# Layer 1's last k-tile and three of layer 0's four k-tiles of the experts' down product in three passes

## The reference

```python
h2 = modulate(rmsnorm(x, norm2_g[l]), sh2, sc2)        # layer 0: context rows too
eidx, w = route(h2, router_w, router_b)
out[tokens of e] += w * ((silu(xblk @ w1[e]) * (xblk @ w3[e])) @ w2[e])

def route(h, router_w, router_b):
    s = sigmoid(h @ router_w)                          # (tokens, 16 experts)
    sb = s + router_b
    gscore = top_k(sb.reshape(n, 4, 4), 2)[0].sum(-1)  # the two best of each group of 4
    # the best group; of its experts the two best, weighted by s
```

## Time and profile before

| | us |
|---|---|
| median of 3 runs (lowest to highest) | 3127.07 (3122.99 to 3132.42) |
| the profiled execution | 3131.46 |
| its span, first to last instruction | 3129.7 |
| mean granted TensorE clock | 0.982 |
| PE busy in the span | 3004.1 (96%) |
| DVE busy | 1785.8 (57%) |
| POOL, ACT busy | 946.6, 929.6 |

### The profile page before, as it was taken

One profiled execution on the slowest core, in us unless ns is written; L12 is line 12 of the kernel. 1 busy time (PEld: TensorE's weight loads), 2 busy tenths in 40 slices (PEclk: granted clock), 3 DMA queues, 4 the chain that ended last, 5 costly groups with the idle time before them and its releaser, 6 DMA issues. The chain is left out here.

```text
span 3129.7 us, 47079 instructions
## 1 busy us (share of the span) xinstructions
PE 3004.1 (96%) x16162; PEld 2410.8 (77%) x16163; DVE 1785.8 (57%) x2568; ACT 929.6 (30%) x1766; POOL 946.6 (30%) x559
## 2 busy tenths in 40 slices
PE   7999899999999989999998999899999998899998
PEld 4887788888888777777776888788888877666665
DVE  5473377858863677535574666365233247899540
ACT  4321265111212342222222422255222134222222
POOL 0050000002222236656574023000012213578664
PEclk9999999999999989999999999999999998999999
DMA  6122342434434448767786512242111144989653
GB/s 274 58 88 78 97 132 88 150 101 148 140 98 184 147 162 275 228 195 238 242 309 224 196 73 91 68 147 76 42 51 51 61 168 165 352 326 375 232 181 81
DMA packets 163516, 499.86 MB, mean 160 GB/s; under 512 B 30634, under 2 KB 83082, under 8 KB 139020
## 3 DMA queue, kind: packets, MB, share of 16 engines
q1 hardware_dynamic: 117288, 393.08, 34.0%
q0 software_dynamic: 17568, 59.82, 8.3%
q10 hardware_dynamic: 28516, 45.03, 4.5%
HBM read 421.76 MB, written 76.44 MB: 159 GB/s over the span
## 5 line engine op out<-in xcount | busy, mean ns | idle before, releaser
L225 PE MATMUL wide<-part,part 128*128 128x512 f32 (+2 forms) x2480 | 972.6, 392 | 18.1 <-DVEq L2552 5.6
L227 PE MATMUL wide<-part,part 128*128 128x512 f32 (+2 forms) x2480 | 950.8, 383 | 0.0
L226 PE MATMUL wide<-part,part 128*128 128x512 f32 (+2 forms) x2480 | 950.6, 383 | 0.0
L225 PEld LDWEIGHTS wide<-part,part 128*128 128x128 f32 x2480 | 469.1, 189 | 116.6 <-issue 22.0
L227 PEld LDWEIGHTS wide<-part,part 128*128 128x128 f32 x2480 | 468.6, 189 | 92.4
L226 PEld LDWEIGHTS wide<-part,part 128*128 128x128 f32 x2480 | 469.3, 189 | 90.5 <-issue 4.8
L1992 POOL TENSOR_TENSOR place<-place,place 128x512 f32 (+3 forms) x80 | 123.1, 1539 | 1019.7 <-DVE place L1939 1019.7
L3060 DVE TENSOR_TENSOR part<-place,part 128x2048 fp32r<-128x2048 f32 x118 | 331.7, 2811 | 4.0
L225 PE MATMUL bank<-part,part 128*128 128x512 f32 (+1 forms) x884 | 327.4, 370 | 3.3 <-DVE part L3080 3.3
L227 PE MATMUL bank<-part,part 128*128 128x512 f32 (+1 forms) x884 | 315.8, 357 | 0.0
L226 PE MATMUL bank<-part,part 128*128 128x512 f32 (+1 forms) x884 | 315.5, 357 | 0.0
(11 more groups left out here) (319 smaller groups left out, 3988.5 us busy)
## 6 DMA issues: line engine op xcount, KB each, us to landing
place<-in_w SPq DMA_DIRECT2D x148, 1024.0 KB, 5.1
place<-in_w SPq DMA_DIRECT2D x22, 2048.0 KB, 10.1
place<-in_ada_w ACTq DMA_DIRECT2D x72, 512.0 KB, 3.8
place<-in_w_gates SPq DMA_DIRECT2D x32, 640.0 KB, 5.0
place<-in_bias SPq DMA_DIRECT2D x96, 192.0 KB
place<-in_ada_w SPq DMA_DIRECT2D x6, 2048.0 KB, 17.4
place<-in_w_rows SPq DMA_DIRECT2D x6, 2048.0 KB, 9.8
place<-in_w_gates SPq DMA_DIRECT2D x16, 768.0 KB
```

The lines of the kernel that those rows point to most:

```text
L225: pe.matmul(out, left[0], right[0], start=first, stop=False)
L226: pe.matmul(out, left[0], right[1], start=False, stop=False)
L227: return pe.matmul(out, left[1], right[0], start=False, stop=last)
```

## The change

- Down products: layer 0 has one plain k-tile and three split ones (before two and two), layer 1 three plain and one split (before four plain). `plain_tiles` and `down_parts` give the numbers and the places.
- With it layer 1 gets layer 0's machinery: `load_second` on SP, `split_second` on DVE (once behind `leave_second`, then behind each expert's four pieces), the second copy on ACT, `leave_gated` on POOL, and its order on PE (gated transposes ahead of the slots').
- In layer 0 `load_second` and `split_second` handle 3 tiles (1.5 MB, 128x3072), in layer 1 one tile (0.5 MB, 128x1024).
- End of layer 0: `scale1` is made ahead of the last two of three pieces of next-layer weights, which now both wait for PE's last down product.
- The load of the second block's token list moves from SP to the head of ACT's queue.
- `keep_turning` ahead of layer 1's `turn(0)`: 10 instead of 40.
- Router: the two best of a group are found with fewer chained DVE operations; `rank` issues its product with the counts of earlier tiles ahead of the wait for the present ones; the first block's rows lose the raw copy.

```diff
-                keep_turning(s, pe, banks[4], 40)
+                keep_turning(s, pe, banks[4], 10)
...
-                do(dve.tensor_tensor(hi, g[:, :, 0:2], g[:, :, 2:4], ALU.max))
-                do(dve.tensor_tensor(both, g[:, :, 0:2], g[:, :, 2:4], ALU.add))
-                do(dve.tensor_tensor(top, hi[:, :, 0], hi[:, :, 1], ALU.add))
-                do(dve.tensor_tensor(mark, both[:, :, 0], both[:, :, 1], ALU.max))
-                do(dve.tensor_tensor(top, top, mark, ALU.max))
...
+                dve.tensor_tensor(sums[:, :, 4:6], twice[:, :, 0:2], twice[:, :, 2:4], ALU.add)
+                do(dve.tensor_tensor(sums[:, :, 0:4], twice[:, :, 0:4], twice[:, :, 1:5], ALU.add))
+                do(dve.tensor_reduce(top, sums, AX.X, ALU.max))
...
+def plain_tiles(last):
+    return 3 if last else 1
+def down_parts(s, last):
+    n = DE // P - plain_tiles(last)
+    at = A_W13 + 32768 + 2 * plain_tiles(last) * D
+    return s["place"](at, n, D), s["part"](at, n, D), s["part"](at + n * D, n, D)
...
             def load_second(e, before):
                 sp.wait_ge(s_y, before * 2 + 2)
                 apart(sp, s_sp)
-                sp.dma_start(down_raw, s["a"]["w2"][layer, e][:, 2:4]).then_inc(s_down, 16)
+                sp.dma_start(down_raw, s["a"]["w2"][layer, e][:, PLAIN:]).then_inc(s_down, 16)
...
-                if e >= 2 and not last:
+                if e >= 2:
                     load_second(e - 1, before)
...
             leave_second()
+            if last:
+                dve.wait_ge(s["first_w2"], 32)
+                split_second(1)
...
-                    if not last:
-                        dve.wait_ge(s_down, (e - 1) * 16 + 16 * n)
-                        split_second(e + n)
+                    dve.wait_ge(s_down, (e - 1) * 16 + 16 * n)
+                    split_second(e + n)
...
-                    if i:
-                        dve.wait_ge((s_room, s_ended)[i - 1], 1)
-                    if i == 2:
+                    if i == 1:
                         scale_next()
+                        dve.wait_ge(s_room, 1)
+                        dve.wait_ge(s_ended, 1)
```

More of the change, by code:

```diff
@@ L2082, in mix_and_route @@
     w13 = place(A_W13, 2, 2 * KD, DE)
-    w2 = place(A_W13 + 32768, 2, DE // P, D)[:, 0] if last else place(A_W13 + 32768, 2, 2, D)[:, 0]
-    w2_second = place(A_W13 + 36864, 2, D)
+    w2, w2_second = place(A_W13 + 32768, 2, plain_tiles(last), D)[:, 0], down_parts(s, last)[0]
     s_w0 = sem("w13_loaded")
@@ L2175, in _ @@
                 sp.wait_ge(s_xb[0], 16)
-            sp.dma_start(w2, s["a"]["w2"][layer, 0][:, 0:4 if last else 2]).then_inc(s["first_w2"], 16)
-            if not last:
-                sp.dma_start(w2_second, s["a"]["w2"][layer, 0][:, 2:4]).then_inc(s["first_w2"], 16)
+            sp.dma_start(w2, s["a"]["w2"][layer, 0][:, 0:plain_tiles(last)]).then_inc(s["first_w2"], 16)
+            sp.dma_start(w2_second, s["a"]["w2"][layer, 0][:, plain_tiles(last):]).then_inc(s["first_w2"], 16)
             if last:
@@ L2414, in _ @@
             act.wait_ge(s_fhi, 4)
[L2415 removed]
+            act.wait_ge(s_fx, 2)
         @block.vector
@@ L2685, in experts @@
     g2 = [place(at + 2 * DE, DE), place(A_W13 + 40960, DE)]
[L2686 to L2689, removed]
+    PLAIN = plain_tiles(last)
+    gtlo, gthi = part(at + 3 * DE, 4, P), part(A_W13 + 41472 if last else at + 2 * DE, DE // P - PLAIN, P)
+    down_a = place(A_W13 + 32768, 2, PLAIN, D)
+    down_raw, down_lo, down_hi = down_parts(s, last)
     plan = s["plan"]
@@ L2696, in experts @@
     s_whi, s_split = sem("w13_hi"), sem("w13_split")
[L2697 to L2700, removed]
+    s_down, s_dhi, s_dsplit, s_glo = sem("w2_second_loaded"), sem("w2_second_hi"), sem("w2_second_split"), \
+        sem("gated_lo")
+    s_ended = sem("products_passed")
     s_xb = s["slots_loaded"]
@@ L2757, in load_w2 @@
             def load_w2(e):
[L2758 to L2761, removed]
+                sp.dma_start(down_a[:, e % 2], s["a"]["w2"][layer, e][:, 0:PLAIN]).then_inc(s_w2[e % 2], 16)
             def load_second(e, before):
@@ L2797, in _ @@
                 if e == 1:
-                    sp.wait_ge(s["first_w2"], 16 if last else 32)
+                    sp.wait_ge(s["first_w2"], 32)
                     sp.sem_inc(s_w2[0], 16)
@@ L2808, in _ @@
             follow_w2(EXP - 1, older)
-            if not last:
-                done = sp.value_load(plan[0:1, PLAN_BEFORE + EXP:PLAN_BEFORE + EXP + 1], min_val=0, max_val=MAXB + 2)
-            if not last:
+            done = sp.value_load(plan[0:1, PLAN_BEFORE + EXP:PLAN_BEFORE + EXP + 1], min_val=0, max_val=MAXB + 2)
+            if last:
+                load_second(EXP - 1, done)
+            else:
                 for s_product in (s_h1, s_h3):
@@ new lines, in down @@
+                split = pe.snap(e + 1)
+                pe.wait_ge(s_dsplit, split)
+                pe.wait_ge(s_glo, r * 2 + (b + 1))
+                for h in range(2):
+                    cols = slice(h * 512, (h + 1) * 512)
+                    for k in range(PLAIN, DE // P):
+                        mm = split_product(pe, banks[6 + h][:], (gthi[:, k - PLAIN, :], gtlo[:, k, :]),
+                                           (down_hi[:, k - PLAIN, cols], down_lo[:, k - PLAIN, cols]), False,
+                                           k == DE // P - 1)
@@ L3009, in copy_gated @@
                 act.activation(gt.rearrange("p a b -> p (a b)"), banks[4][:], ACT.Copy).then_inc(s_gc, 1)
-                if not last:
-                    act.activation(gthi.rearrange("p a b -> p (a b)"), banks[4][:, 256:512], ACT.Copy).then_inc(s_gc, 1)
+                act.activation(gthi.rearrange("p a b -> p (a b)"), banks[4][:, PLAIN * P:512], ACT.Copy).then_inc(s_gc, 1)
             def copy_y(r, b):
@@ L3026, in body @@
                     silu(r * 2 + (b + 1))
[L3027 to L3028 removed]
                     copy_gated(r, b)
[L3030 to L3031 removed]
+                    copy_turned(0, b, r * 2 + (b + 2))
                     copy_h3(r * 2 + (b + 1))
@@ L3204, in body @@
                 for b in range(2):
-                    if not last:
-                        leave_gated(r, b)
+                    leave_gated(r, b)
                     leave_turned(0, b, r * 2 + (b + 2))
@@ L3216, in _ @@
             R = pool.snap(used // 2)
-            if not last:
-                leave_gated(R, 0)
+            leave_gated(R, 0)
             add_block(R, 0)
```

91 lines of the change are left out of this document (35 added, 56 removed).

## The result

| | before | changed |
|---|---|---|
| median | 3128.74 us (4 runs) | 3169.49 us (4 runs, 3167.79 to 3177.46) |
| ratio, 95% interval | | 1.0138 (1.0124 to 1.0153) |
| profiled execution's span | 3129.7 | 3167.8 |
| PE busy | 3004.1 | 2999.4 |
| DVE busy | 1785.8 | 1868.9 |

The medians lie 41 us apart, the profiled spans 38; the ratio, of the means, stands for 43. The direction was right, the size wrong by 30 us; 3169 lies outside the range of 3121 to 3152. In the span PE is busy 5 us less and idle 43 us more, and part of its busy time runs slower.

The account below looks back on a forecast made before the run. PE bound the kernel, with DVE full where layer 1's single-block experts follow each other. -10.0 + 15.0 + 1.9 - 8.2 + 14.0 - 1.6 = + 11.1 us took the median from 3127.07 to 3138, range 3121 to 3152.

Parts of the forecast that it names:

- What PE saves: Down products: 0.36 us saved per block, -10.0 us over layer 0's 28 blocks and -8.2 over layer 1's 23.
- behind an expert of two or three blocks nothing is lost, 10 of 15 times: Layer 0: split parts ready 12.1 us after their tiles' issue (T), PE wanting them at 13.7, so no wait.
- - 3.5 us, three such places: Layer 0, behind single-block experts 3, 7 and 11: PE waits 3.5 us each for the split parts.
- + 4.5 more: Layer 0, parts of expert 13, second single in a row: PE waits 5.4 us, 4.5 more than before.
- The clock: PE at half clock after long waits: three could cost 1.5 us each, counted only in the upper bound.
- high end: Upper bound, sum + 22 us: slower half MB, longer tile split and subtraction (+ 5 and + 3), and the clock.
- waits 14: Layer 1: PE waits near 14 us for DVE's pieces, at experts 3 to 6 and 10, 11; sum + 14.0.
- They still come ahead of DVE: Layer 1: SP's pieces, issued up to 13 us later, still land before DVE reaches them, at T + 6 earliest.
- Rival 3: Layer 1: transfers become the bound, nine singles losing 1 to 2 us more each, 3151 us; chance 0.15 with the clock.
- Rival 1: DVE's disturbance by POOL shrinks as PE slows, half of 29 us of waits goes, 3124 us; chance 0.25.
- Router and idle products: Router and start: -0.8 us per layer, -1.6; fewer idle products at layer 0's end give 1 within + 1.9.
- rival 2: DVE hides everything, only PE's work counts: -18.2 - 1.6 - 3 (idle products), 3104 us; chance 0.08.

Follow-up runs that it names:

- e6: Changed kernel, POOL's low-part subtraction cut to 8 of each tile's 128 columns in both layers: layer 0's stage 495.3 us against the changed kernel's 507.7.
- e4: Changed kernel, DVE making parts of only two of layer 0's three split tiles from the second expert on: layer 0's stage 487.3 us against 507.7.
- e5: As e4, with only those two tiles loaded as well (1 MB instead of 1.5): layer 0's stage 480.6 us against the changed kernel's 507.7.
- e3: Changed kernel with layer 0 back at two plain and two split k-tiles, layer 1 keeping three plain and one split: 3130.7 us, 1.0012 of before.
- e7: Changed kernel with 28 idle products ahead of PE's wait for the parts of layer 0's very last block: 3165.5 us, 1.0132 of before.
- e9: e3, but in layer 1 DVE makes no parts of w2 after the first expert's; loads stay: 3128.4 us, 0.9996 of before.
- e10: e9, also without layer 1's load of w2's split tile after the first expert's and SP's wait ahead of it: 3116.3 us, 0.9958 of before.
- e1: Changed kernel with the old down products and their orders in both layers, the small edits kept: 3117.6 us, 0.9966 of before.
- e12: e1 with the 40 idle products of before ahead of layer 1's first transposes: 3126.2 us, 0.9995 of before.

## Why the prediction was wrong

- **What PE saves: right.** A half-body without a wait took 18.05 us in layer 0 and 18.78 in layer 1 (37.55 for two), as forecast to 0.03.
- **Layer 0, "behind an expert of two or three blocks nothing is lost, 10 of 15 times": wrong, small.** The parts were ready at T + 14.0 where PE wants them at T + 13.7. Nine short waits of 0.15 to 1.05 us, each with some 0.25 more because the first split record no longer overlaps the last plain one.
- **Layer 0, "- 3.5 us, three such places", "+ 4.5 more": the step that failed.** Its two terms were mis-sized. Waits of the split parts came to 23.7 us against 15.9 (15.0 more than before's 0.9): 6.47 for experts 4 and 8 where 3.5 was forecast, 6.47 for expert 13 where 5.4 was, and for expert 12 1.58 and another 1.96 for pieces, where 3.5 was. At expert 8 DVE's chain from T of expert 7 to the ready parts was 3.8 us longer than forecast: 1.4 by the first transfer (copy at T + 8.2, not T + 6.8), 0.7 and 1.8 by the two splits, which were priced undisturbed (5.3) and took 6.0 and 7.1. So the operations' error counts twice, once in the expert ahead, the transfer's once; PE's own block was 0.7 slower, which leaves the 3.0 us. That POOL stretches the operations is shown by e6, the shares of DVE's time and of the transfer by e4 and e5.
- **The clock: put at nothing in the sum, priced as a bound.** The three long waits were followed by 1.8, 2.6 and 2.6 us of loss with the clock at 0.50, and three of layer 1's shorter waits by the same clock; the forecast had it at its high end only (and that end, + 11.1 + 5 + 3 + 4.5, is + 23.6, not + 22). In stage 0 the sum is closed: 26 blocks at 18.05 are 469.3; the waits of all kinds are 27.5, the half clock 7.0, and 3.9 are left, which I put down to the short waits' restarts: 507.7. The forecast had 469.3 and 15.9. So of the 22.5 us that it missed in this stage, 11.6 are waits, 7.0 the clock behind the long ones, 3.9 the rest.
- **Layer 1, "waits 14": 18, near; the half clock behind some of them wasn't in it.** In e3 and e7, with the same layer 1, the waits are 13.1 and 12.9 us, so 14 is within what executions differ by. The half clock is 5.4 us over experts 1 to 5, and 2.9 over 7 to 10, restarts included. DVE took 87.5 us from the last subtraction of expert 2 to that of expert 6 (ends 2737.43 and 2824.98), 84.9 forecast; PE had lost 2.4 us before the first of them already.
- **"They still come ahead of DVE": true only because DVE was late.** The late loads on SP are a second limit right behind DVE's (e9, e10). Rival 3 named it and then counted it as one with the transfers' rate; in the changed kernel the rate wasn't it (share 0.90, below before's 1.02).
- **Rival 1 (disturbance shrinks): wrong sign.** POOL's new operation adds to it (e6: -12.4 us without).
- **Router and idle products: -10.6 measured (e1), -4.6 forecast** (-1.6, and -3 by rival 2; behind the longer last block the sum gave the idle products 1). By whole times 9 of the 10.6 go with the 30 idle products (e12 0.9995, e1 0.9966), of which only 4.5 can be placed; what the router and the rest give, 1.5 us, isn't told from nothing (0.9984 to 1.0006). The parts of the span don't tell more: up to the first T, where these kernels differ in little but two blocks' down products, the profiled executions reach from 7.5 us less than before's (e12) to 1.8 more (e5).

What stays open: why one execution of the split layer 1 takes 466.8 us and another 460. PE's waits from 2690 us on, e3 and then e7, against the eleven of 18.0 us above:

```profile
PE wide L225 <- DVE part L3053: 13.1, 8, 2.4
```

```profile
PE wide L225 <- DVE part L3055: 12.9, 8, 2.4
```

It doesn't go with layer 0's k-tiles: e7 has them and e3 doesn't. The executions of one kernel spread as far (e7's four from 3160.3 to 3171.8 us, its profiled one the shortest; e3's twelve from 3124.5 to 3143.2). So of layer 1's + 16.3 in the table of the result about 10 are the k-tile as e3 and e7 show it; the whole times of e3 and e1 give 14. What makes the two kinds of execution no run shows.

## What to carry to other kernels

An engine that is full in a stretch, though nobody waits for it yet, is the bound of any edit that adds to it: price what the edit adds with the durations of that stretch, allow for the neighbour's work that stretches it, and count it once for each time that it stands in the chain ahead of the wait. A long wait of PE costs itself and the half clock behind it. Before a difference of a few us between two profiles is explained, look for a second profile of the same instructions. When an engine is relieved and little comes back, look for who waits next: here a load that had been moved behind a wait.

## What the runs showed of the hardware

- Behind waits of PE of 6.5 and 7.1 us the granted clock was 0.50 for 3 to 5 us each time; with idle products in the 7.1 us it wasn't (e7). Behind waits of 2.4 us it went either way: in the changed kernel it fell at 2761, 2826 and 2948 us and didn't at 2738, 2803 and 2925. In e7 it fell behind such waits at 2736, 2801 and 2920 and didn't at 2779. The changed kernel's three stood 22 us behind another such wait, but e7's at 2920 stood 118 us behind one, so that isn't the condition; what is, the traces don't show.
- A DVE subtraction of 128x2048 took from 2.29 to 6.60 us in layer 1 (3.2, 4.2 and 4.8 between), the copy from 1.21 to 2.73. Each of the subtractions longer than 2.29, 38 of 58, overlapped an elementwise operation of POOL by 1.1 us or more; some of 2.29 did too. With POOL's new operation cut short, the casts of 128x3072 had a mean of 1.84 us instead of 2.27 (e6), and the subtractions' mean stayed (4.19 and 4.15).
- A plain product ahead of a wait lost its overlap with the next record: two of them cost 1.88 us there.
